# One encoder layer on one core: attention hands its high and low parts over before the exponentials and scales probabilities a tile later, and the last norm's root lives in PSUM

## The reference

```python
s = (einsum(q_nope, k_nope) + einsum(q_rope, k_rope)) * scale      # 1024 queries x 1040 keys, per head
p = softmax(s, axis=-1)
a = einsum(p, v)
...
ff = (silu(hn @ w_gate) * (hn @ w_up)) @ w_down
h = h + ff * rsqrt(mean(ff * ff) + EPS) * g_ffn_post
```

## Time and profile before

| | us |
|---|---|
| runs, median (lowest, highest of 3) | 2333.02 (2331.67, 2337.22) |
| profiled execution, its own time | 2335.76 |
| its span in the profile | 2334.0 |
| TensorE busy in the span | 2205.8 (95%) |
| VectorE, ScalarE, GpSimd busy | 1065.7, 917.3, 461.0 |

### The profile page before, as it was taken

One profiled execution on the slowest core, in us unless ns is written; L12 is line 12 of the kernel. 1 busy time (PEld: TensorE's weight loads), 2 busy tenths in 40 slices (PEclk: granted clock), 3 DMA queues, 4 the chain that ended last, 5 costly groups with the idle time before them and its releaser, 6 DMA issues. The chain is left out here.

```text
span 2334.0 us, 32080 instructions
## 1 busy us (share of the span) xinstructions
PE 2205.8 (95%) x11716; PEld 1845.5 (79%) x11716; DVE 1065.7 (46%) x1727; ACT 917.3 (39%) x1454; POOL 461.0 (20%) x213
## 2 busy tenths in 40 slices
PE   5999999999999999889999998789999999999996
PEld 4988888888888888677777776667888788878785
DVE  5003665665764754366666665373533001421102
ACT  4213354354354453544444443444343223222222
POOL 3110000000000000111111111114444444444443
PEclk8999999999999999999999999899999999999998
DMA  3211112111111111211111110542333233343233
GB/s 142 75 63 64 33 60 64 40 59 63 40 59 56 40 57 40 107 41 46 46 45 45 45 45 28 193 145 89 94 132 98 92 108 108 116 136 99 90 104 122
DMA packets 78714, 182.61 MB, mean 78 GB/s; under 512 B 6864, under 2 KB 27664, under 8 KB 78128
## 3 DMA queue, kind: packets, MB, share of 16 engines
q1 hardware_dynamic: 78640, 181.61, 23.9%
HBM read 152.09 MB, written 29.49 MB: 78 GB/s over the span
## 5 line engine op out<-in xcount | busy, mean ns | idle before, releaser
L1798 POOL TENSOR_TENSOR w_lo<-w_raw,w_hi 128x1024 fp32r<-128x1024 f32 x136 | 331.1, 2435 | 398.9 <-ACT w_hi L1807 398.9
L83 PE MATMUL h_bank<-hn_hi,w_hi 128*128 128x512 f32 (+2 forms) x952 | 374.1, 393 | 3.9 <-PEq L165 2.5
L84 PE MATMUL h_bank<-hn_lo,w_hi 128*128 128x512 f32 (+2 forms) x952 | 356.8, 375 | 0.0
L85 PE MATMUL h_bank<-hn_hi,w_lo 128*128 128x512 f32 (+2 forms) x952 | 356.3, 374 | 0.0
L83 PE MATMUL f_bank<-ffn_in_hi,w_hi 128*128 128x512 f32 x768 | 303.5, 395 | 16.7 <-DVE ffn_in_lo L1987 10.9
L85 PE MATMUL f_bank<-ffn_in_hi,w_lo 128*128 128x512 f32 x768 | 301.8, 393 | 0.0
L84 PE MATMUL f_bank<-ffn_in_lo,w_hi 128*128 128x512 f32 x768 | 301.8, 393 | 0.0
L83 PEld LDWEIGHTS h_bank<-hn_hi,w_hi 128*128 128x128 f32 x952 | 179.6, 189 | 36.7 <-issue 9.9
L85 PEld LDWEIGHTS h_bank<-hn_hi,w_lo 128*128 128x128 f32 x952 | 179.4, 188 | 29.8
L84 PEld LDWEIGHTS h_bank<-hn_lo,w_hi 128*128 128x128 f32 x952 | 179.6, 189 | 28.1 <-issue 3.8
L1807 ACT CAST w_hi<-w_raw 128x1024 fp32r<-128x1024 f32 x136 | 142.5, 1048 | 130.7 <-PE f_bank L85 127.9
(11 more groups left out here) (330 smaller groups left out, 4360.5 us busy)
## 6 DMA issues: line engine op xcount, KB each, us to landing
w_raw<-in_w_ffn SPq DMA_DIRECT2D x136, 512.0 KB, 3.6
w_raw<-in_w_hgrn SPq DMA_DIRECT2D x54, 512.0 KB, 3.6
w_raw<-in_w_out SPq DMA_DIRECT2D x15, 512.0 KB, 4.0
w_raw<-in_w_head SPq DMA_DIRECT2D x9, 512.0 KB, 5.7
X<-in_x SPq DMA_DIRECT2D x8, 520.0 KB, 6.5
values<-v_stage SPq DMA_DIRECT2D x32, 128.0 KB, 1.7
values_h<-values SPq DMA_DIRECT2D x8, 512.0 KB, 4.9
gate_out<-raw SPq DMA_DIRECT2D x8, 512.0 KB, 2.9
```

What stands on the lines that cost most here:

```text
L83: pe.matmul(out, wh, xh, start=start, stop=False)
L84: pe.matmul(out, wh, xl, start=False, stop=False)
L85: return pe.matmul(out, wl, xh, start=False, stop=stop)
L1798: pool.tensor_tensor(w_lo[i][:], w_raw[i][:], w_hi[i][:].bitcast(F32), ALU.subtract).then_inc(w_lo_done, 1)
```

## The change

- Attention, ScalarE: in each step both high parts come before the exponential.
- Attention, VectorE: in each step low(2j+3) follows `find_shift(j)` directly, and `normalize` runs for the tile before (j-1); the last tile's `normalize` moves into the next segment, after piece 2 (kind 0) or piece 5 (kind 1).
- The last norm: `rs` of `inverse_rms` lies in PSUM bank 0 (`rs_bank`), free in the FFN; GpSimd adds tiles 0, 1, 2, 4 and 6 and VectorE 3, 5 and 7; the set with Ln and Exp is loaded before the second half's down projection.

```diff
@@ attention, ScalarE
                         if cur is not None:
                             high(cur, 2 * j + 2)
+                            if 2 * j + 3 < TILES:
+                                high(cur, 2 * j + 3)
                         if nxt is not None:
                             softmax(nxt, j)
-                        if cur is not None and 2 * j + 3 < TILES:
-                            high(cur, 2 * j + 3)
@@ attention, VectorE
                 def segment(cur, nxt, p, which):
+                    after = 2 if which == 0 else OF_SEGMENT[1][0]
                     if p is not None:
                         for i in OF_SEGMENT[which]:
                             piece(p, i)
+                            if i == after and cur is not None:
+                                normalize(cur, QS - 1)
+                    elif cur is not None:
+                        normalize(cur, QS - 1)
...
                         if nxt is not None:
                             find_shift(nxt, j)
-                            normalize(nxt, j)
                         if cur is not None and 2 * j + 3 < TILES:
                             low(cur, 2 * j + 3)
+                        if nxt is not None and j:
+                            normalize(nxt, j - 1)
@@ output and FFN
-        gate_bank, up_bank, y_bank, sum_bank = bank[4], bank[5], bank[6:8], bank[2]
+        gate_bank, up_bank, y_bank, sum_bank, rs_bank = bank[4], bank[5], bank[6:8], bank[2], bank[0]
-        BY_POOL = [1, 3, 5]
+        BY_POOL = [0, 1, 2, 4, 6]
@@ inverse_rms
-                    act.activation(rs[:], sum_bank[:], ACT.Ln, bias=t.gain("eps", 0), scale=1.0 / D
+                    act.activation(rs_bank[:], sum_bank[:], ACT.Ln, bias=t.gain("eps", 0), scale=1.0 / D
                                    ).then_inc(rs_done, 1)
                     act.wait_ge(rs_done, 2 * s + 1)
-                    act.activation(rs[:], rs[:], ACT.Exp, scale=-0.5).then_inc(rs_done, 1)
+                    act.activation(rs_bank[:], rs_bank[:], ACT.Exp, scale=-0.5).then_inc(rs_done, 1)
@@ ScalarE, after the second half's hidden tiles
                 act.wait_ge(stored, 16)
+                act.preload_act_table_set("natural_log_exp_and_others")
                 pairs(act, 1, down(1))
@@ finish and the last scales: in1=rs[:] becomes in1=rs_bank[:]
```

More of the change, by code:

```diff
@@ L1977, in finish @@
                     gain = t.gains[:, bass.ds(pair.index() * 2 + (GAINS["ffn_post"] + i), 1)]
-                    dve.scalar_tensor_tensor(out=y[:, m, :], in0=y[:, m, :], scalar=gain, in1=rs[:].unsqueeze(1),
+                    dve.scalar_tensor_tensor(out=y[:, m, :], in0=y[:, m, :], scalar=gain, in1=rs_bank[:].unsqueeze(1),
                                              op0=ALU.mult, op1=ALU.mult).then_inc(f_scaled, 1)
@@ L2101, in _ @@
                         dve.scalar_tensor_tensor(out=y[:, m, :], in0=y[:, m, :], scalar=t.gain("ffn_post", m),
-                                                 in1=rs[:], op0=ALU.mult, op1=ALU.mult).then_inc(f_scaled, 1)
+                                                 in1=rs_bank[:], op0=ALU.mult, op1=ALU.mult).then_inc(f_scaled, 1)
                     if m and m - 1 not in BY_POOL:
```

## The result

| | before | after |
|---|---|---|
| median of runs, us (lowest to highest) | 2333.72 (2331.67 to 2337.22, 4 runs) | 2297.35 (2296.09 to 2298.90, 4 runs) |
| profiled execution, us | 2335.76 | 2298.90 |
| its span, us | 2334.0 | 2297.1 |
| ratio of the times, 95% interval | | 0.9845 [0.9832, 0.9859] |

The kernel became 36.4 us faster, 1.55%. The forecast was 2301 with a range of 2295 to 2311. By the trace 34.1 us came from attention (from the table load ahead of it to the one ahead of the output projection: 485.85 to 451.72) and 4.2 from the end of the kernel. Attention began 1.5 us later than before; its start lies between 971.6 and 976.4 in the traces of this study, whatever was edited, so this is a variation between executions. Output projection (117.06 and 117.05) and FFN up to the last addition to the sum of squares (737.40 both times) kept their lengths.

The account below looks back on a forecast made before the run. TensorE was taken to set the pace in attention (441 of 478 us busy, about 37 us waits). Attention 29.5 plus the end 3.5 made 33 us; with 1 us kept back, 2333.0 - 32 = 2301 us, range 2295 to 2311.

Parts of the forecast that it names:

- The final products: Attention: TensorE's 30 waits of the value product for VectorE's low part go, 1.56 us in most segments; 22.8 us.
- The last two full segments: Attention: turn(0) there needs normalize(3), done about 7.6 us after step 3's head scores start, against 8.9; saves 1.27 each.
- Step 2's excess: Attention, step 2: 4.95 us against a plain 4.67, turn(7) waiting for low(5); the 0.28 goes in 15 segments, 4.2 us.
- `k_nope_lo`: Attention: the first query piece's projection no longer waits for k_nope_lo, which stood behind normalize(3); 4.3 us go.
- The first segment: Attention, segment without products: tail scores 2 start about 1.0 us earlier, normalize leaves the circle of scores, shift, exponential; 2.1 us.
- The new wait: Attention, seven kind-1 segments: normalize(3) behind q_nope_lo delays turn(0) from 4.20 to 4.80 us; -0.55 us each, -3.9 us.
- The end: Last norm: no table load between Ln and Exp saves 1.3 us, scales and additions 2.2; together 3.5 us.
- The preload's cover: FFN: the early 1.28 us table load fits into the 3 us before TensorE wants the weights; costs nothing, without cover 1.3.
- B: Rival, attention step 3: v_lo or w_lo holds shift(2) longer, low(8) comes too late; costs 10 us, 2311; chance 0.14.
- C: Rival, last norm: a PSUM operand doesn't free the scales, 14.4 us instead of 9.2; 2306; chance 0.07.
- D: Rival, attention: the waits only change place, such as turn(0) waiting for normalize(3) in every segment; 2329.5; chance 0.04.
- E: Rival, attention, slower: exp(j) behind high(2j+3) comes too late for the next step's tail scores; 2347 if 2.5 us later; chance 0.03.

## Why the prediction was right, point by point

**The final products, 22.8 us.** The mechanism was right, the size 25.1: H3 to the next segment fell by 1.97 in seven segments of kind 0 and 1.58 in six of kind 1 (23.3, against 13 x 1.56 = 20.3), and by 0.95 and 0.87 behind the last two full segments (1.8, against 2.5). The 3.0 more in these thirteen were not in the prediction's steps at all. The first matmul after a wait is followed by the second only 0.34 us later (1179.83 and 1180.17 in before), after transposes 0.31 to 0.32 later, within an unbroken run after 0.23 (1141.36, 1141.59 above). A stall that goes takes this restart with it. Of the 144 groups that multiply by the values, 143 began with such a gap in before and 113 in after: 26 of the 30 belong to these thirteen segments, 26 x 0.11 = 2.9 us.

**The last two full segments** gave 0.7 less than predicted. This step of the prediction failed: it let only operations with two SBUF inputs stand, and the scaling has one. VectorE, GpSimd and TensorE of after in order of time:

```profile
1383.18 1.60 DVE L1401 TENSOR_SCALAR raw<-raw,inv 128x1040 f32<-128x1040 f32 x1
```
```profile
1382.96 1.26 POOL L1258 TENSOR_TENSOR mixed<-mixed,rec 128x512 f32<-128x512 f32 x1 [5.94 <-DVE mixed L1441]
```
```profile
1384.84 1.97 PE L1527 MATMUL a_bank<-consts,raw 128*128 128x128 f32 x8 [2.94 <-DVE raw L1401]
```

normalize(3) now comes right behind the gating and so beside GpSimd's addition; it takes 1.60 instead of 0.76 and turn(0) waits for it. The longest scaling in before was 0.77. Without the 0.84 us of holding turn(0) would have come at about H3+7.17, earlier than the 7.6 of the prediction, so two errors partly cancel here. The Trainium skill (SBUF — State Buffer, "Who interferes with whom") says that `tensor_scalar` can enter a two-port mode, in which it contends with GpSimd for the pair of ports that they share. The prediction used only its sentence on two inputs. This trace and the kernel with VectorE's order alone agree with it for 1040 columns (1.60 and 2.96); the one-column `tensor_scalar` of the shift stayed at 0.22.

**Step 2's excess, 4.2.** 4.5: 4.96 became 4.66 in 15 segments.

**`k_nope_lo`, 4.3.** 5.0, the first segment's share counted in: the query piece comes 0.63 us earlier in each of seven segments, and 0.09 more is its restart, which goes with the wait.

**The first segment, 2.1.** 2.1, once the share of the `k_nope_lo` term in the segment after it is taken out: tail scores 3 come 1.0 us earlier and the exponential that the third key piece (piece 2) waits for another 1.0. shift(2) took 2.00 us there. The number needed luck: in three of the five traces with the same attention (attention alone, root in SBUF, no preload) the granted clock fell to 0.5 to 0.6 for some 3 us behind the wait of 2.3 us in that segment, and 0.9 us of the gain was lost; in after it stayed at 1.00.

**The new wait, -3.9.** -2.7: turn(0) came 0.53 later (0.60 expected), and the fold gave 0.15 back (0.05 expected), 0.05 before it and 0.10 behind it. The kernel with normalize(3) ahead of piece 5 has 2.8 for the same term.

These five make 34.0 of attention's 34.1 us. The stretch behind the last turn(0) is as long as before; it varies by 1.7 us over five traces with the same attention code.

**The end, 3.5.** 4.2: the table load 1.28, as predicted, and 0.07 from the root's move into PSUM, where no change had been taken; scales and additions 11.42 to 8.55, that is 2.9 instead of 2.2. "What matters is the reader" held (root in SBUF: +3.9), but it was the whole of it: the new division of the additions, which the sum counted on, gives nothing.

**The preload's cover** held: the load at 2158.42 lay ahead of a weight block that GpSimd finished in time, and FFN kept its length.

**Rivals.** B: low(8) had 0.56 us to spare, not 0.3, and was never late. C is refuted by the eight scales at 0.74. D: only the seven waits of 0.38 and 0.6 us more in each of the two behind the last full segments came in the place of the 30. E: no exponential was waited for within a step of the 15 segments with products (the three waits of the first segment stood in before too); its order did matter the other way, as the kernel with VectorE's order alone shows.

The forecast was 3.65 us above the median. 1 us was kept back without need, attention gave 4.6 more than its sum and the end 0.7 more; 1.5 us went the other way by the later start of attention, and 1.2 lie in the medians, since that of before is now 0.7 higher and the change of the span 0.5 larger than that of the medians. The larger part of attention's surplus is the restart of the matmul groups and the cheaper new wait, less the held scaling. Part of the closeness is therefore luck; the waits that were named did go, for the reasons given.

## What to carry to other kernels

When an operation is moved ahead of a wait in one engine's order, look at the other engine that feeds the same consumer: here one move alone gives nothing, the other alone costs 38 us, and both together gain 34. Before an SBUF operation of VectorE is moved, lay out what GpSimd does at its new place, also if it has a single wide input. And read terms of one or two microseconds from the length of the stage: starts of stages and the granted clock behind long waits vary by as much from one execution to the next.

## What the runs showed of the hardware

- A group of 512-column matmuls has 0.34 us between its first two starts after a wait and 0.31 to 0.32 after transposes, against 0.23 within a run (before, 144 groups): 0.11 us a restart after a wait.
- A VectorE `tensor_scalar` over 1040 fp32 columns with one SBUF tensor is held by a GpSimd operation on SBUF (0.76 us becomes 1.60 to 1.71 beside an addition of 1.26 to 1.29 and 2.96 beside a subtraction of 2.40); over one column it isn't (0.213 to 0.217 in 15 that ran wholly beside GpSimd).
- ScalarE's Ln of 512 columns out of PSUM takes 0.66 us into PSUM and 0.69 into SBUF; Exp takes 0.58 with both ends in PSUM and 0.63 with both in SBUF. The Trainium skill (ScalarE: Activation LUTs, "Step-by-step: what each stage is for") calls PSUM the faster destination; the trace agrees.
- Behind a wait of 2.94 us the granted clock fell to 0.54 for 3 us in one execution and stayed at 1.00 in another, with the same instructions around it; it made 1.4 us. Behind the first segment's wait of 2.3 us it fell in three traces of the change's attention and stayed at 1.00 in two, which made 0.9 us.
